# Four steps moved in the order of a chunked delta-rule scan

## The reference

```
def step(S, inp):
    r_t, w_t, k_t, v_t, a_t, b_t = inp
    sa = jnp.einsum('bhvk,bhk->bhv', S, a_t)
    S = (S * w_t[:, :, None, :] + sa[..., None] * b_t[:, :, None, :]
         + v_t[..., None] * k_t[:, :, None, :])
    return S, jnp.einsum('bhvk,bhk->bhv', S, r_t)

# a = -kk, b = kk * rate, kk = unit vector of k * k_k
# bonus = sum(r * k * r_k) over the head's channels, times v
```

## Time and profile before

| | |
|---|---|
| median of three runs | 1810.77 us |
| the profiled execution | 1810.77 us, span 1809.0 us |
| TensorE busy over the span | 1772.9 us (98%) |
| VectorE | 1252.4 us (69%) |
| ScalarE | 946.1 us (52%) |
| GpSimd | 323.5 us (18%) |
| the chain that ended last, share on TensorE | 37% of the span, VectorE 4%, ScalarE 1% |
| the six pairs | from 188.2 to 359.2 us |

### The profile page before, as it was taken

How to read it: one execution, slowest core, us unless ns; L and a number is a source line. 1 busy time by engine, 2 the same in 40 slices (tenths; PEclk the granted TensorE clock), 3 DMA queues, 4 the chain that set the end, 5 groups by cost and what they waited for, 6 DMA issues and landing times. The chain is left out here.

```text
span 1809.0 us, 37312 instructions
## 1 busy us (share of the span) xinstructions
PE 1772.9 (98%) x15389; PEld 1543.7 (85%) x15389; DVE 1252.4 (69%) x1913; ACT 946.1 (52%) x1670; POOL 323.5 (18%) x359
## 2 busy tenths in 40 slices
PE   8999999999999999999999999999999999999998
PEld 6777888868999988878886698999999988999997
DVE  5346777667777676567568578677777887777776
ACT  6633444445644445345379566544445865444454
POOL 3012577723200000000034104000006040000000
PEclk9999999999999999999999999999999999999999
DMA  6322000103333333272300222333334113333331
GB/s 197 94 70 70 26 4 4 36 2 94 94 97 114 96 114 104 67 150 85 94 1 1 70 71 70 105 105 105 106 117 132 56 36 106 105 105 105 104 101 65
DMA packets 152252, 148.27 MB, mean 82 GB/s; under 512 B 13692, under 2 KB 150042, under 8 KB 152090
## 3 DMA queue, kind: packets, MB, share of 16 engines
q1 hardware_dynamic: 151964, 145.91, 26.2%
q10 hardware_dynamic: 126, 0.04, 0.0%
HBM read 143.84 MB, written 2.10 MB: 81 GB/s over the span
## 5 line engine op out<-in xcount | busy, mean ns | idle before, releaser
L1855 DVE TENSOR_TENSOR weight_low<-weight_ring,weight_high 128x1024 fp32r<-128x1024 f32 (+2 forms) x250 | 253.8, 1023 | 148.3 <-ACT weight_high L1843 148.3
L1843 ACT CAST weight_high<-weight_ring 128x1024 fp32r<-128x1024 f32 (+2 forms) x250 | 215.1, 864 | 246.9 <-PE psum L248 116.6
L1890 PE MATMUL psum<-tail_x_high,weight_high 128*128 128x256 f32 x1008 | 282.7, 280 | 0.9 <-DVE weight_low L1855 0.6
L1891 PE MATMUL psum<-tail_x_low,weight_high 128*128 128x256 f32 x1008 | 282.3, 280 | 0.0
L1892 PE MATMUL psum<-tail_x_high,weight_low 128*128 128x256 f32 x1008 | 282.3, 280 | 0.0
L1890 PEld LDWEIGHTS psum<-tail_x_high,weight_high 128*128 128x128 f32 x1008 | 189.7, 188 | 3.2 <-DVE weight_low L1855 0.9
L1891 PEld LDWEIGHTS psum<-tail_x_low,weight_high 128*128 128x128 f32 x1008 | 189.7, 188 | 1.6
L1892 PEld LDWEIGHTS psum<-tail_x_high,weight_low 128*128 128x128 f32 x1008 | 189.6, 188 | 0.0
L246 PE MATMUL psum<-tail_hidden_high,weight_high 128*128 128x512 f32 (+1 forms) x400 | 147.8, 370 | 0.5 <-DVE tail_hidden_low L4052 0.5
L248 PE MATMUL psum<-tail_hidden_high,weight_low 128*128 128x512 f32 (+1 forms) x400 | 147.5, 369 | 0.0
L247 PE MATMUL psum<-tail_hidden_low,weight_high 128*128 128x512 f32 (+1 forms) x400 | 147.4, 368 | 0.0
(11 more groups left out here) (559 smaller groups left out, 4757.8 us busy)
## 6 DMA issues: line engine op xcount, KB each, us to landing
weight_ring<-in_w_ff SPq DMA_DIRECT2D x32, 1024.0 KB, 5.3
weight_ring<-in_ffn_w_gate SPq DMA_DIRECT2D x22, 1024.0 KB, 5.3
weight_ring<-in_ffn_w_up SPq DMA_DIRECT2D x22, 1024.0 KB, 5.4
weight_ring<-in_ffn_w_down SPq DMA_DIRECT2D x32, 512.0 KB, 4.6
weight_ring<-in_rw_in SPq DMA_DIRECT2D x10, 1024.0 KB, 5.3
weight_ring<-in_attn_w_in SPq DMA_DIRECT2D x9, 1024.0 KB, 5.2
weight_ring<-in_ffn_w_down SPq DMA_DIRECT2D x8, 768.0 KB, 4.7
weight_ring<-in_w_out SPq DMA_DIRECT2D x4, 1024.0 KB, 5.1
```

What stands on the lines that cost most here:

```text
L1843: last = act.copy(high, source)
L1855: last = dve.tensor_tensor(low, source, high, ALU.subtract)
L1890: pe.matmul(out, w_hi, x_hi, start=kk == 0 and not more, stop=False, skip_group_check=more)
L1891: pe.matmul(out, w_hi, x_lo, start=False, stop=False, skip_group_check=more)
```

## The change

Four things are moved; no tensor operation is added or removed, and what is computed stays.

- Start of a pair: on TensorE `turn1` goes ahead of `ab`; on ScalarE the copy `tok0` goes ahead of `ab0` and `ab1`; on VectorE the two `rb` go ahead of the two `inv`.
- ScalarE, level 4: `root` of the next pair goes ahead of the copy of x of head 1 (`keep_x(1, 4)`).
- VectorE: `read_key` is merged into `unit_key`, so `rk` of the next pair is made right behind `kk`, after level 4, and no longer after level 5. In `front` the two already stood together.
- TensorE: `bonus_sum` of the next pair goes ahead of `wu0` and `wu1`.

```
 def main_steps():
-    pe = ["b", "turn0", "ab", "turn1", "k", ...
+    pe = ["b", "turn0", "turn1", "ab", "k", ...
-    act = ["ab0", "ab1", "tok0", "tok1", ...
+    act = ["tok0", "ab0", "ab1", "tok1", ...
-    dve = [... ("inv_T", "inv_T_eye", "inv", "rb", "aks") ...
+    dve = [... ("inv_T", "inv_T_eye", "rb", "inv", "aks") ...
@@ unit_key
         dve_p.did("kk", dve.scalar_tensor_tensor(kk, ...
-
-    def read_key(dve, p):
         pe_p.wait(dve, "kk_sum", p)
         dve_p.wait(dve, "k_new", p)
         dve_p.did("rk", dve.scalar_tensor_tensor(rk_sum[:], ...
@@ main, ScalarE
+                keep_tok(0)
                 for e in range(2):
                     pe_s.wait(act, "ab", p)
                     pool_s.wait(act, f"below5_{e}", p, 1)
                     act_s.did(f"ab{e}", act.copy(ab[e][:], low(bank_x[e])))
-                keep_tok(0)
                 keep_tok(1)
...
                 keep_x(0, 4)
-                keep_x(1, 4)
                 if prep_next:
                     root(act, p + 1)
+                keep_x(1, 4)
@@ main, VectorE
                 for e in range(2):
+                    dve_s.did(f"rb{e}", dve.tensor_tensor(rb[e][:], ...
+                for e in range(2):
                     act_s.wait(dve, f"ab{e}", p)
                     dve_s.did(f"inv{e}", dve.tensor_tensor(inv[e][:], ...
-                for e in range(2):
-                    dve_s.did(f"rb{e}", dve.tensor_tensor(rb[e][:], ...
...
                 if prep_next:
-                    read_key(dve, p + 1)
                     against(dve, p + 1)
@@ main, TensorE
                 turn(0)
+                turn(1)
                 act_s.wait(pe, "y", p, 1)
                 dve_s.wait(pe, "q", p, 1)
                 ... ab
-                turn(1)
...
+                if prep_next:
+                    bonus_sum(pe, p + 1)
                 for e in range(2):
                     ... wu
-                if prep_next:
-                    bonus_sum(pe, p + 1)
```

More of the change, by code:

```diff
@@ L330, in main_steps @@
     both = range(2)
-    pe = ["b", "turn0", "ab", "turn1", "k", "x0_1", "x1_1", "turn2", "turn3", "m0_1", "t0_1", "m1_1"]
+    pe = ["b", "turn0", "turn1", "ab", "k", "x0_1", "x1_1", "turn2", "turn3", "m0_1", "t0_1", "m1_1"]
     for lv in range(2, 6):
@@ L335, in main_steps @@
     pe += ["wu0", "wu1", "out"]
-    act = ["ab0", "ab1", "tok0", "tok1", "x0_1", "x1_1", "tok2", "tok3", "x0_2", "x1_2", "a_side", "x0_3", "av", "x1_3", "x0_4", "x1_4",
+    act = ["tok0", "ab0", "ab1", "tok1", "x0_1", "x1_1", "tok2", "tok3", "x0_2", "x1_2", "a_side", "x0_3", "av", "x1_3", "x0_4", "x1_4",
            "x0_5", "x1_5", "wu0", "wu1", "h", "y"]
-    dve = [f"{n}{e}" for n in ("inv_T", "inv_T_eye", "inv", "rb", "aks") for e in both] + ["m0_1", "t0_1", "m1_1"]
+    dve = [f"{n}{e}" for n in ("inv_T", "inv_T_eye", "rb", "inv", "aks") for e in both] + ["m0_1", "t0_1", "m1_1"]
     for lv in range(2, 6):
@@ L904, in _ @@
         pe.wait_ge(placed, heads)
-Scan = namedtuple("Scan", "square still root decays clip decay_sum new_key unit_key read_key against bonus middles scaled_keys reader key_norm bonus_sum begin_act begin_dve begin_pool begin_pe main act_s dve_p pe_s state temps")
+Scan = namedtuple("Scan", "square still root decays clip decay_sum new_key unit_key against bonus middles scaled_keys reader key_norm bonus_sum begin_act begin_dve begin_pool begin_pe main act_s dve_p pe_s state temps")
 def scan_chunks(k, t, passes, mix):
@@ L1170, in main @@
                 for e in range(2):
+                    dve_s.did(f"rb{e}", dve.tensor_tensor(rb[e][:], twos(bank_t[e])[:, :, 1, :], mask(MASK_UPTO_T), ALU.mult))
+                for e in range(2):
                     act_s.wait(dve, f"ab{e}", p)
                     dve_s.did(f"inv{e}", dve.tensor_tensor(inv[e][:], ab[e][:], mask(0), ALU.mult))
-                for e in range(2):
-                    dve_s.did(f"rb{e}", dve.tensor_tensor(rb[e][:], twos(bank_t[e])[:, :, 1, :], mask(MASK_UPTO_T), ALU.mult))
                 for e in range(2):
@@ L1387, in _ @@
             close.load(sp)
-    return Scan(square, still, root, decays, clip, decay_sum, new_key, unit_key, read_key, against, bonus, middles, scaled_keys, reader, key_norm, bonus_sum,
+    return Scan(square, still, root, decays, clip, decay_sum, new_key, unit_key, against, bonus, middles, scaled_keys, reader, key_norm, bonus_sum,
                 begin_act, begin_dve, begin_pool, begin_pe, main, act_s, dve_p, pe_s, state, temps)
```

8 lines of the change are left out of this document (1 added, 7 removed).

## The result

The changed kernel took 1820.54 us (median of five runs, 1819.8 to 1821.7) against 1810.77 us (1810.0 to 1811.1) before: 1.0054 times as long, 95% interval 1.0040 to 1.0069, so 9.8 us slower. 1823.3 was predicted, with 1818.5 to 1827.0 as range. The profiled execution of after took 1820.98 us with a span of 1819.3, 10.3 more than before's 1809.0.

A forecast was written before the change was run, and what follows sets the result against it. The prediction took TensorE to bound the recurrent part, with thin slack before its next group's operand. Its four terms, 1.9 + 3.8 + 3.0 + 3.8 = 12.5 us, added to 1810.8 gave 1823.3 us, range 1818.5 to 1827.

The forecast's parts named there:

- A: Start of a pair: `turn1` delays `ab`; +0.50 us in pairs 2 and 4, +0.3 in three, 0 in pair 0; 1.9 us.
- C: Level 5: `rk` behind `kk` delays the addition `t1_4` that `m1_5` reads; 0.6 us a pair, five pairs, 3.0 us.
- D: End of a pair: `bonus_sum` ahead of `wu0` no longer fills the wait before `out`; 0.76 us a pair, five pairs, 3.8 us.
- B: Level 4: `root` makes the copy of `x1_4` 1.06 us later against 0.30 slack; `m1_4` +0.77 in five pairs, 3.8 us.
- Stalls that give back: TensorE's unexplained stops between `out` and `b` absorb added waits: at most 5.8 us back, likely half, about 1820; chance 0.12.
- The port on `rk`: GpSimd's `b` starts first, `rk` waits about 1.27 us, `m1_5` up to 1 us later in five pairs: 1828; chance 0.08.
- Delays that overlap: Delays within one pair overlap instead of adding: only the largest, 0.8 per pair in five, and the pair's start: 1816.5; chance 0.05.
- Not slower: Level 1 waits for something other than the second cut, and moved operations lie in holes: 1809.6, 1.2 us faster; chance 0.05.

The follow-up runs named there:

- experiment 3: Kernel before with only the activations of `root` put ahead of the copy of `x1_4` on ScalarE: 1.0013 times the time of before.
- experiment 7: Changed kernel with `bonus_sum` put back behind `wu1` on TensorE: 1.0026 times the time of before.
- experiment 1: Kernel before with only `turn1` put ahead of `ab` on TensorE: 1.0007 times the time of before.
- experiment 2: Kernel before with only the two `rb` put ahead of the two `inv` on VectorE: 0.9993 times the time of before.
- experiment 4: Kernel before with only `rk` put directly behind `kk` on VectorE: 1.0016 times the time of before.
- experiment 8: Kernel before with `rb` ahead of `inv` and `rk` made in level 3 on VectorE, ahead of `kk_clip`: 0.9997 times the time of before.
- experiment 9: Kernel before with `rb` ahead of `inv`, and GpSimd waiting for `rk` before `bh` instead of before `kh`: 0.9996 times the time of before.
- experiment 6: Kernel before with `rk` directly behind `kk` and `bonus_sum` ahead of `wu0`, nothing else: 1.0035 times the time of before.

## Why the prediction was right, and where its sum was not

Slower was right, and so was the place: waits of TensorE in the recurrent part, each of those named, with the busy time unmoved. The sum was 12.5 against a core of +11.0 and a median of +9.8. That it came so near is in part luck: A and C were too high by 1.2 and 1.0, D too low by 0.8.

| part | predicted | measured | from |
|---|---|---|---|
| A, start of pair | 1.9 | 0.7 | `turn0` to `av`, before and after |
| B, `root` | 3.8 (0.77 a pair) | 3.8 (0.76) | experiment 3 |
| C, `rk` | 3.0 (0.6) | 2.0 (0.39) | experiment 7 less 3, `av` to `out` |
| D, `bonus_sum` | 3.8 (0.76) | 4.6 (0.92) | after less experiment 7, `av` to `out` |
| sum | 12.5 | 11.0 | unrounded 0.68, 3.79, 1.97 and 4.58; core of after less that of before: 11.0 |

**Part A** was the term with the largest miss. Pair by pair it changed by -0.40, +0.13, +0.41, +0.14, +0.43 and -0.02, where I had 0, 0.3, 0.5, 0.3, 0.5 and 0.3. `turn1` cost the chain nearly what I said (experiment 1). The step that failed was that "`rb` ahead of `inv` fills VectorE's idle 0.28 us ..., so `aks` comes no later than before": I priced it at nothing, because I looked only at what is queued behind it on VectorE. It also decides whether VectorE's `inv` or GpSimd's cut gets its operands first, and shortens the way to level 1 by 0.23 where the cut wins (experiment 2). In after it did in pairs 1, 3 and 5. In pair 0, which I held to be covered by the wait on `aks`, `rb` in front makes `aks` come sooner and takes that very wait away: -0.43 in experiment 2, -0.40 in after. The prediction had both durations in hand, 1.84 beside 1.30, and read from them that the two hinder each other, but used this only for `rk`.

**Part B** held to 0.01 us a pair.

**Parts C and D** held as a sum: 1.36 a pair predicted, 1.31 measured. The split was wrong by one wait. `wu0` had a wait of about 0.2 of its own on the addition of `m0_5`. I saw 0.08 of it and let `bonus_sum` use it, but `rk`, which comes earlier in the pair, had used it all up (experiments 4 and 7). Then `bonus_sum` pays in full, with 0.14 for two more changes of shape that I had left out.

**The range** does not follow from its own rule: half of the stalls' full price is 1820.4, not 1818.5, and the port's price is 1828, not 1827.

**The rivals.** *Stalls that give back:* refuted. Without a cause TensorE stood 6.4 us, before 5.8, and over the ten experiments the part from `out` to the next `turn0` was 25.3 to 27.9 with no relation to the length of the waits (27.9 in experiment 8 with a core like that of before, 26.7 in after with 11 us more). By the traces these are waits for instructions; see the last section. *The port on `rk`:* did not come about in the changed kernel (0.74 for all five), because `rk` started 0.37 ahead of GpSimd's `b` in four pairs and 0.16 in pair 0, where I had computed 0.3; it is `b` that took longer. It is real, though: it met another pair of operations in part A, and `rk` and `bh` in experiments 1 and 2. *Delays that overlap:* refuted but for the 0.2 a pair between C and D. *Not slower:* refuted; the copy of `x1_4` was late by more than its slack, and `m1_4` came 0.7 late in each of five pairs. `turn1` next to `turn0` saved nothing that shows (experiment 1).

On the port the Trainium skill (SBUF — State Buffer, section on who interferes with whom) says that a VectorE operation with two SBUF inputs and a GpSimd operation that reads SBUF exclude each other, and that the one issued first goes first. The traces agree: with `bh` 0.15 ahead `rk` took 1.67 (experiment 2), with `rk` 0.06 ahead it took 0.74 and `bh` 1.81 (before). The two together took 1.82 and 1.87, where 0.74 and 1.27 one after the other make 2.01, so they overlap by a little. VectorE's `rb`, which reads one input from PSUM, took 0.75 for two operations in both orders.

**Still open.** Why one stop of TensorE between two pairs takes 0.8 us and another 1.9, and whether `rk` in level 3 together with the wait of experiment 9 would add up to a gain that can be measured. No version here beats the kernel before beyond its uncertainty.

## What to carry to other kernels

When one engine sets the pace with nothing to spare, moving an operation "into a hole" of another engine is judged by the operation queued behind it: compare its length with the slack of the next group, and the excess goes straight to the total. Add such prices in the order of the program, and use each existing wait only once, for the first edit that reaches it. An operand moved earlier on the fast engine saves nothing if its consumer on the bound engine is also moved out of a wait that it used to fill: `rk` and `bonus_sum` together cost 7.2 us (experiment 6). And an edit that seems free on one of two engines that hinder each other must be held against the other's starts.

## What the runs showed of the hardware

- Of two operations of VectorE and GpSimd that start together here, the one that starts first, even by 0.03 to 0.06 us, keeps its time and the other pays: `rk` took 0.74 alone or first, 1.67 when it started 0.15 behind `bh` and 1.80 when it started 0.03 behind; the two cuts took 1.60 first and 1.83 second, and `inv` beside them 1.65 and 1.29. So an edit elsewhere that shifts one start past the other can make an operation 1.1 us longer, and `out` behind it came 0.6 late (experiment 2, pair 1).
- TensorE stops once between each two pairs, in the run of small matmuls of `out` and `b`, with no operand missing by the profile. Counted in its own records (matmuls and weight loads), each of the twelve kernels stops at the same five places, whatever was moved ahead of them, and these lie 1792, 1536, 1792 and 1536 records apart, that is 7 or 6 times 256. The stop in `b` of pair 2, with 15 of its 32 records left, in before and in after:

```profile
246.67 0.66 PE L1253 MATMUL psum<-front_ar,front_bh 64*64 64x128 f32 x15 [0.97 <-issue]
```

```profile
250.09 0.66 PE L1249 MATMUL psum<-front_ar,front_bh 64*64 64x128 f32 x15 [1.00 <-issue]
```

- All 60 stops end 1.2 to 1.6 us after a transfer of 16 KB on the queue that the profile calls instruction has ended, and 2.2 to 3.0 us after its start. The 256 records up to a stop take 1.9 to 2.1 us without it and every other 256 records of this part 3.3 or more. By this they are waits for instructions in the densest stretch, though no run changed the supply itself. In after each of these transfers starts behind the added waits, 1.0 to 1.9 us after the start of `out`, which is why the waits gave nothing back. The Trainium skill (Runtime: NRT & Kernel Launch, section on instruction fetch mechanics) has the fetch of instructions mostly hidden behind execution; that holds for the other blocks here, and not for these five.
- The five stops sum to 5.7 us (experiment 1) to 7.9 (experiment 8), from the start of one record to the next, and with them varies the part from `out` to `turn0`, by 2.6 us between kernels that do the same work there. So a difference of the core of 1 us (experiment 9) can drown in the medians, and that is likely why the larger ones are there only to within 2 us (experiment 3: core +3.8, median +2.0).
